# Four weight loads of a decoder layer moved ahead of its row loop, and the first block's schedule shifted by three rows

## The reference

```
z    = x @ W_in                                   # 9 sections of 1024 columns
o_A  = hgrn2_chunkwise(q, k, v, log f)            # 8 heads of 128
y_B  = cb * causal_depthwise_conv3(cc * ch)
mix  = (sigmoid(ga) * (o_A @ W_a) + sigmoid(gb) * (y_B @ W_b)) @ W_out
x1   = LayerNorm(alpha * x + mix)
x2   = LayerNorm(alpha * x1 + peer(x1))
out  = x2 + sigmoid(x2 @ W_pg) * (p @ W_pp)

peer(x1): for each token and each of 8 heads
  query = x1 @ W_q (2 halves of 128); scores against 2 x 128 keys
  top 16 of each half, 256 sums, top 16 of these -> 16 experts of 16384, softmax weights g
  result += sum_k g_k * gelu(u[e_k] . x1) * v[e_k]
```

## Time and profile before

| | |
|---|---|
| median of 3 runs | 1816.69 us (1812.79 to 1818.82) |
| the profiled execution | 1813.96 us |
| its span, first to last instruction | 1812.2 us |
| PE, DVE, ACT, POOL busy | 87%, 70%, 41%, 27% of the span |
| mean granted PE clock | 0.982 |
| moved by DMA | 655.37 MB, 362 GB/s over the span |

### The profile page before, as it was taken

One profiled execution on the slowest core, in us unless ns is written; L12 is line 12 of the kernel. 1 busy time (PEld: TensorE's weight loads), 2 busy tenths in 40 slices (PEclk: granted clock), 3 DMA queues, 4 the chain that ended last, 5 costly groups with the idle time before them and its releaser, 6 DMA issues.

```text
span 1812.2 us, 16782 instructions
## 1 busy us (share of the span) xinstructions
PE 1575.9 (87%) x4960; PEld 871.2 (48%) x4960; DVE 1275.4 (70%) x2750; ACT 747.9 (41%) x1899; POOL 496.0 (27%) x528
## 2 busy tenths in 40 slices
PE   8999989999999998889888668788787878877787
PEld 7888878776555566444344223332222223322224
DVE  4454475388998999678878876876666687666653
ACT  6566672222132224444334334444444443444432
POOL 0000000022222223233334433433333333333330
PEclk9999999999999999999999989999999999999999
DMA  5112368899999999999999999999999999999993
GB/s 203 70 65 93 113 262 343 294 415 398 421 420 421 417 397 418 406 415 412 421 421 411 422 416 422 391 420 423 421 412 422 410 410 422 421 421 422 420 418 138
DMA packets 94788, 655.37 MB, mean 362 GB/s; under 512 B 10352, under 2 KB 14192, under 8 KB 17008
## 3 DMA queue, kind: packets, MB, share of 16 engines
q0 software_dynamic: 73728, 536.90, 71.7%
q1 hardware_dynamic: 20976, 117.48, 16.7%
HBM read 652.24 MB, written 2.10 MB: 361 GB/s over the span
## 4 chain that ended last, share of the span: by engine, by line
PE 50%; DMA 30%; DVE 8%; ACT 8%; issue 3%; POOL 0%; SPq 0%; POOLq 0%; DVEq 0%; ACTq 0%
DMA uv<-in_pk_uv,idx 28%; PE psum L1703 12%; PE psum L1609 11%; PE psum L1467 10%; PE psum L1628 5%; DVE uv L1319 4%; PE psum L1671 4%; PE psum L1642 2%; PE psum L1580 2%; ACT diag L867 2%; ACT coef L859 1%; ACT L855 1%; ACT L833 1%; DMA raw<-in_w_in 1%; PE psum L1733 1%
## 5 line engine op out<-in xcount | busy, mean ns | idle before, releaser
L1703 PE MATMUL psum<-uv,diag 128*128 128x512 f32 x1440 | 721.0, 630 | 209.7 <-ACT diag L867 206.3
L632 POOL DMA_INDIRECT uv<-in_pk_uv,idx x512 | 493.6, 964 | 1279.8 <-PE psum L1703 583.1
L1319 DVE CUSTOM_DVE_ANT_0 uv<-uv,psum 128x1024 f32<-128x1024 f32 x512 | 623.2, 1218 | 310.5 <-DMA uv<-in_pk_uv,idx 304.1
L1703 PEld LDWEIGHTS psum<-uv,diag 128*128 128x128 f32 x1440 | 258.9, 195 | 644.8 <-ACT diag L867 426.8
L855 ACT ACTIVATE gelu<-dots 128x1 f32<-128x1 f32 x512 | 103.6, 202 | 780.7 <-DVE dots L1319 778.4
L1609 PE MATMUL psum<-xT,raw 128*128 128x384 f32 x640 | 208.1, 486 | 0.0
L1332 DVE SCALAR_TENSOR_TENSOR oT<-uv,coef,oT 128x1024 f32<-128x1024 f32 x148 | 189.3, 1279 | 3.0 <-ACT coef L859 3.0
L1609 PEld LDWEIGHTS psum<-xT,raw 128*128 128x128 f32 x640 | 120.9, 190 | 82.2
L859 ACT ACTIVATE coef<-gelu,weight 128x1 f32<-128x1 f32 x512 | 150.9, 295 | 16.6
L867 ACT ACTIVATE diag<-ident,coef 128x128 f32<-128x128 f32 x360 | 144.6, 402 | 11.8
L1467 PE MATMUL psum<-xTh,w_hi 128*128 128x512 f32 x256 | 105.0, 410 | 2.6 <-DVE xTl L1046 2.6
(11 more groups left out here) (204 smaller groups left out, 1576.7 us busy)
## 6 DMA issues: line engine op xcount, KB each, us to landing
raw<-in_w_in SPq DMA_DIRECT2D x40, 1024.0 KB, 7.8
raw_a<-in_w_a SPq DMA_DIRECT2D x12, 1024.0 KB, 4.7
raw<-in_pk_w_q SPq DMA_DIRECT2D x10, 1024.0 KB, 9.1
raw<-in_w_branch_a SPq DMA_DIRECT2D x8, 1024.0 KB, 8.0
raw<-in_w_branch_b SPq DMA_DIRECT2D x8, 1024.0 KB, 9.0
uv<-in_pk_uv,idx POOLq DMA_INDIRECT x512, 10.3
raw<-in_w_out SPq DMA_DIRECT2D x6, 1024.0 KB, 9.6
raw_w<-in_pk_w_q SPq DMA_DIRECT2D x6, 1024.0 KB, 6.0
```

The costliest lines, as they stand in the source:

```text
L632: pool.indirect_dma_start(uv[:, r % UV, :], None, pk_uv, bass.IndirectOffsetOnAxis(idx[:, i % 2, j:j + 1], 0)).then_inc(row_in[r % UV], 16)
L1319: V.tensor_tensor_reduce(u, u, x_cur[:], 1.0, 0.0, ALU.mult, ALU.add, dots[:, r % 32:r % 32 + 1]).then_inc(dot_done, 1)
L1703: last = T.matmul(B[i][:], diag[:, n % DR, :], uv[:, r % UV, D + i * 512:D + (i + 1) * 512], start=(r in FIRST), stop=(k == BLOCK_ROWS - 1 ...
```

## The change

Eight units, 4 to 11 (loads 2 to 5 before), are loaded as three transfers by `tri_fetch` behind query load 2 of block 0: three units into `gaT[:, :, 128:]`, three into `gbT[:, :, 128:]`, two into a part of `scores`. The host lays their columns out as `w_tri`. PE reads these units from there. The remaining unit loads are 6 to 19: load 6 where load 2 was, load 7 where load 3 was, load 8 where load 4 was. Load 9 waits for unit 15, loads 10 and 11 for unit 17, and load n from 12 on for unit 2(n - 3) + 1 as before. Query load 3 is issued with the third transfer, ahead of load 6.

The 38 late units are spread over 61 rows; merges and outputs start 3 rows later with the same spacing, so the last output row is 96. The norms and transposes keep their distance to it. `Q0` lies one row behind the last transpose rather than two, query 1 takes 5 rows instead of 6, and the scores of queries 0 and 1 come one row behind instead of two. Search 8 does three steps in a row instead of two. Of the rows behind the outputs, 106 isn't shared any more.

```diff
+        TRI0 = 4
+        tri = [gaT[:, :, P:], gbT[:, :, P:], scores[:, 0, :, P:3 * P]]
+        TRI1 = TRI0 + 8
...
             if i == PKH:
-                return [SCORE_ROW[0] + 2 + k // 2 for k in range(STEPS)]
+                return [SCORE_ROW[0] + 2 + k // 3 for k in range(STEPS)]
...
-        UNIT_ROW += [[(UNIT_MM * n + i) * 58 // (UNIT_MM * (len(UNITS) - EARLY)) for i in range(UNIT_MM)]
+        UNIT_ROW += [[(UNIT_MM * n + i) * 61 // (UNIT_MM * (len(UNITS) - EARLY)) for i in range(UNIT_MM)]
                      for n in range(len(UNITS) - EARLY)]
-        MERGE_ROW = [58 + n * 23 // 128 for n in range(16 * KT)]
-        OUT_ROW = [83 + n * 11 // 96 for n in range(4 * (TB - 1) * KT)]
+        MERGE_ROW = [61 + n * 23 // 128 for n in range(16 * KT)]
+        OUT_ROW = [86 + n * 11 // 96 for n in range(4 * (TB - 1) * KT)]
...
-        Q0 = TURN_ROW[-1] + 2
-        QUERY_ROW = [[Q0 + (n * 5 // 16 if h == 0 else 6 + n * 6 // 16 if h == 1 else 17 + 14 * (h - 2) + n * 9 // 16)
+        Q0 = TURN_ROW[-1] + 1
+        QUERY_ROW = [[Q0 + (n * 5 // 16 if h == 0 else 5 + n * 5 // 16 if h == 1 else 17 + 14 * (h - 2) + n * 9 // 16)
                       for n in range(2 * KT)] for h in range(PKH)]
-        SCORE_ROW = [QUERY_ROW[h][-1] + 2 for h in range(PKH)]
+        SCORE_ROW = [QUERY_ROW[h][-1] + (1 if h < 2 else 2) for h in range(PKH)]
...
-                return r % 3 == 1 and 106 <= r <= 120
+                return r % 3 == 1 and 109 <= r <= 120
...
-        LOADS += [(("unit", n), n - 2 if n < 4 else (n - 2) % 3) for n in range(2, len(UNITS) // 2)]
+        LOADS += [(("unit", n), n - TRI1 // 2 if n < 9 else (n - 8) % 3) for n in range(TRI1 // 2, len(UNITS) // 2)]
...
+            def tri_fetch(j):
+
+                sp.dma_start(tri[j], w_tri[j, :, :, 0:tri[j].shape[2]]).then_inc(tri_in[j], 16)
...
             fetch(pk_w_q[2], "query", 0, 2)
+            sp.wait_ge(t_done, USE["z", len(Z_PARTS) - 1] + 1)
+            tri_fetch(0)
+            tri_fetch(1)
+            sp.wait_ge(t_done, USE["query", 0, 0, 1] + 1)
+            fetch(pk_w_q[3], "query", 0, 3)
+            tri_fetch(2)
             sp.wait_ge(t_done, USE["unit", 1] + 1)
-            unit_fetch(2)
-            for h in (3, 4, 5):
+            unit_fetch(TRI1 // 2)
+            for h in (4, 5):
                 sp.wait_ge(t_done, USE["query", 0, h - 3, 1] + 1)
                 fetch(pk_w_q[h], "query", 0, h)
             sp.wait_ge(t_done, USE["unit", 3] + 1)
-            unit_fetch(3)
+            unit_fetch(TRI1 // 2 + 1)
...
-            for n in range(4, len(UNITS) // 2):
-                if n == 4:
+            for n in range(TRI1 // 2 + 2, len(UNITS) // 2):
+                if n == TRI1 // 2 + 2:
                     sp.wait_ge(t_done, USE["query", 0, 5, 1] + 1)
-                elif n < 7:
-                    sp.wait_ge(t_done, USE["unit", 2 * (n - 3) + 1] + 1)
                 else:
-                    sp.wait_ge(t_done, USE["unit", 2 * (n - 3) + 1] + 1)
+                    sp.wait_ge(t_done, USE["unit", 2 * max(n - 3, min(n - 2, 8)) + 1] + 1)
                 unit_fetch(n)
-                if n == 8:
+                if n == 9:
                     sp.wait_ge(t_done, USE["query", 0, PKH - 1, 1] + 1)
-                if 8 <= n < 8 + TB:
-                    first_parts(n - 7)
+                if 9 <= n < 9 + TB:
+                    first_parts(n - 8)
...
-                    pe.wait_ge(*loaded("unit", n // 2))
+                    if TRI0 <= n < TRI1:
+                        pe.wait_ge(tri_in[(n - TRI0) // 3], 16)
+                    else:
+                        pe.wait_ge(*loaded("unit", n // 2))
```

More of the change, by code:

```diff
@@ L30, with build @@
 CW = 2 * P
-def build(nc, x, x_t, p_t, w_a, w_in, vec_cols, w_branch_a, w_branch_b, w_out,
+def build(nc, x, x_t, p_t, w_a, w_in, w_tri, vec_cols, w_branch_a, w_branch_b, w_out,
           ln1_g, ln1_b, pk_w_q, sub_keys_t, pk_uv, ln2_g, ln2_b, ple_w_gate, ple_w_proj, out):
@@ L208, in build @@
         xT_in = sem("xT_in")
+        tri_in = [sem(f"tri_in{j}") for j in range(len(tri))]
         yc0_step, yc0_done, mix_step = sem("yc0_step"), sem("yc0_done"), sem("mix_step")
@@ L1605, in unit_mm @@
                         pe.wait_ge(xT_in, 16)
-                    pe.wait_ge(*loaded("unit", n // 2))
+                    if TRI0 <= n < TRI1:
+                        pe.wait_ge(tri_in[(n - TRI0) // 3], 16)
+                    else:
+                        pe.wait_ge(*loaded("unit", n // 2))
                     t_free(r)
-                half = n % 2
-                last = T.matmul(B[bank(r)][:, 0:SEQ - P], slot(SLOT["unit", n // 2])[:, k, half * P:half * P + P],
+                if TRI0 <= n < TRI1:
+                    w, part = tri[(n - TRI0) // 3], (n - TRI0) % 3
+                else:
+                    w, part = slot(SLOT["unit", n // 2]), n % 2
+                last = T.matmul(B[bank(r)][:, 0:SEQ - P], w[:, k, part * P:part * P + P],
                                 xT[:, k, P:], start=(k == 0), stop=(k == KT - 1), skip_group_check=True)
@@ L1869 @@
     w_a = w_in[[1, 0, 2, 3]].reshape(4, -1, P, w_in.shape[3], 2, P).transpose(0, 1, 2, 4, 3, 5)
+    sections = [(sect, c) for pair in range(4) for sect in (6, 5, 4) for c in (2 * pair, 2 * pair + 1)][4:12]
+    columns = [w_in[sect, c // 2][:, :, c % 2 * P:c % 2 * P + P] for sect, c in sections]
+    columns.append(columns[-1])
+    w_tri = _np.stack([_np.concatenate(columns[3 * j:3 * j + 3], axis=2) for j in range(3)])
     laid = {
@@ L1875 @@
         "w_in": w_in[4:],
+        "w_tri": w_tri,
         "vec_cols": _np.concatenate([_columns(given[name]) for name in
```

## The result

The changed kernel takes 1829.29 us (median of 6 runs, 1826.49 to 1832.23) against 1814.88 us before: 1.0075 times, 95% interval 1.0063 to 1.0087. That is 14.4 us slower, where 1809.9 us was forecast. The profiled execution is the slowest of the six (1832.23 us, span 1830.5), 18.3 us above the profiled one of before.

What follows compares the result with a forecast made beforehand. The DMA is full, but PE's fixed work paces the rows up to 705 us and gathers alone thereafter. Terms -7.5 + 0.3 + 0.4 = -6.8 us took the median 1816.69 to 1809.9 us; range 1805.5 to 1817.0.

Steps and rivals of the forecast that it cites:

- rival E: Unit stage: loads 9 and 10 take 16.0 us each, PE stands 5.7 us twice; 5.9 us slower, 1822.6 us; chance 0.09.
- PE ends the output chunks at 705 us again, but with row 96 in place of row 93 behind it: From 366 to 705 us: PE's fixed work ends unchanged with 3 more rows beneath it, the main term, 7.5 us less.
- It just fits by the sum.: From 340 to 366 us, ahead of the rows: at 421 GB/s the DMA has room for the 4.19 MB more.
- Rival D: Start of the rows: at 362 GB/s only 2.65 MB fit, query 4 is 4.2 us late; 1813.4 us; chance 0.07.
- I take 0.3 us late; bounds 0 and 4.2 us.: Start of the rows: query load 4, reckoned to land at 365.3 us with 0.8 us margin, costs 0.3 us.
- VectorE starts behind by 2 us and has 8.7 us of free time ... to make it good.: First dots to 455 us: VectorE's late start of 2 us is absorbed in 8.7 us of free time, without PE waiting.
- After, with a DMA that is not full, some 27 can be landed by then.: By 455 us: some 27 gathers landed, leaving 52.4 MB against 52.2 MB to 579 us, a lag under a microsecond.
- rival B: From 400 to 455 us: the ring of six buffers is full and the DMA idles; 1813.0 us; chance 0.14.
- So both make it by 0.4 us.: Unit stage: loads 9 and 10, with leads cut to 10.3 us, land just in time; 0.4 us taken for both.
- Behind 705 us, 3 rows fewer are to be gathered, ... 7.5 us less.: Behind the output chunks: 3 rows fewer at 2.49 us each, 7.5 us less.
- Rival C, VectorE becomes the bound: Rows before 705 us: VectorE's 9 us of added work is hidden only by half, 4 us lost; 1813.3 us; chance 0.08.
- I cost all this at nothing, bounds -1 and +2.5 us.: End of block 0: closer queries and denser search 8 stay hidden, at no cost, bounds -1 and +2.5 us.

Runs made afterwards that it cites:

- rows_only: The kernel before with the change's 61 unit rows, later merges and outputs and drawn-together end of block 0, but the old loads: 1820.25 us, 1.0028.
- tail_only: The kernel before with only the end of block 0 (queries, scores, search 8) drawn together as in the change: 1818.23 us, 1.0022.
- late58x: The kernel before with the new loads, query load 4 right behind query load 3, third transfer and load 6 behind query load 7: 1816.35 us, 1.0011.
- late61: The change with third transfer, load 6 and four half loads moved behind query load 7, query load 4 right behind query load 3: 1818.39 us, 1.0022.
- loads_only: The kernel before with the change's three early transfers and shorter leads, but the old rows and end of block 0: 1821.54 us, 1.0036.
- late58: As late58x, with the four half loads (x of blocks 1 to 3, norm gain) also issued right behind query 7: 1815.01 us, 1.0001.
- late59: As late58, with 59 unit rows instead of 58, and merges and outputs one row later: 1814.92 us, 1.0004.

## Why the prediction was wrong, point by point

The change came out slower, at 1829.29 us, where the range ended at 1817.0 us and even rival E gave only 1822.6. The main step that failed is "PE ends the output chunks at 705 us again, but with row 96 in place of row 93 behind it": they ended at 720.9 us, as PE began its late units late and waited 8.3 us for VectorE's merge of row 85. The points below follow the prediction from the start of the rows on.

**"It just fits by the sum."** The first step that failed. It reckoned with 421 GB/s ahead of the rows; the stretch moved 368. At that rate the room is (368 - 260) x 26 = 2.8 MB, not 4.19. More than half of the (421 - 368) x 26 = 1.4 MB that are missing lies before the new loads could flow: from 340 to 344 us the DMA moved 223 GB/s, as in the kernel before (225), since the first transfer is issued only at 342.74 us. That is (421 - 223) x 4 = 0.8 MB. The 374 GB/s of the first two transfers make 0.4 MB. Rival D had about the right price here (362 GB/s, 2.65 MB) and too small a chance, but partly by luck: its 362 GB/s mixed the end of two gain loads with pieces of 512 B, landed by 328.0 us, with a load of 8 KB runs; the load with 1.5 KB pieces had landed at 319.4 us. The Trainium skill (DMA: Bandwidth & Descriptors, Bandwidth, "Where 436 GB/s comes from") has 358 GB/s for one core's loads from HBM. The 374 GB/s of the first two transfers lie near it, but loads with 8 KB runs ran at 421 in the same kernel, so its limit is not what the trace shows. The size of the pieces fits, with `xT`'s 372 GB/s beside it (two loads agree; no run changed the size alone).

**"I take 0.3 us late; bounds 0 and 4.2 us."** Query 4 landed at 371.40 us where 365.3 was reckoned, and PE waited 3.9 us. That is within the bound. Of the 6.1 us, 2.3 were there when the second transfer landed, 1.6 came up to the third (364.3 us), and 2.2 with query 4 itself, which took 4.7 us behind load 6 with gathers under way, where 2.5 was reckoned. What the bound left out is the clock: the query took 6.56 us for 3.74 at a granted clock of 0.53 from 370 to 375 us, 2.8 us more. The late units began 8.1 us later; 6.7 are these two, the rest lay ahead of 366 us.

**"VectorE starts behind by 2 us and has 8.7 us of free time ... to make it good."** It started 3.4 us behind. The free time was not free in the way needed: VectorE waits for PE's convolution units there (6.8 us, one wait of 4.5; 2.6 was the longest before), and the ring of six rows was full meanwhile (POOL waited up to 7.8 us for VectorE's sum).

**"After, with a DMA that is not full, some 27 can be landed by then."** Only 26 were issued by 455 us, against 27 before, and 24 had landed. From 420 to 440 us the DMA left (421 - 273) x 10 + (421 - 145) x 10 = 4.2 MB unmoved, as much as the change took out of the rows. This is rival B's idling, and with it the 455 to 579 us stretch was again full, with more in it: rows 34 to 59 waited 14.7 us for their gathers, where it was 10.1 before, and took 89.9 us for 84.2. The budget of bytes was right as a sum and wrong in the place: a ring of six buffers can't store what the DMA has to spare.

**"So both make it by 0.4 us."** Right, for loads 9 and 10: 9.3 and 9.5 us of 10.3, and no wait on PE. The 0.4 us of the sum were nothing, and load 9 was issued 8 us later than reckoned.

**The merges.** The prediction read the chain as "three pieces without a break". The 1.28 us of "issue" between the merges and the output chunks were a break, and it is the one that grew. The prediction costed merges and outputs as keeping "their density" and named no wait. The largest single term was here: PE's wait for VectorE's last merge, 8.3 us against 1.3, because row 85 isn't reached when PE has done the same work. Its dot began at 673.07 us, 14.4 us later than row 82's before (658.70), and the merges ended only 7.2 us later. Without the new loads (rows_only) the wait was still 5.9 us, so most of it comes from the three rows themselves. With 1.7 us of slower output chunks behind the wait, its 7.0 us more make 8.7 us of the 16.0 by which the outputs end late; 7.2 are from the start.

**"Behind 705 us, 3 rows fewer are to be gathered, ... 7.5 us less."** This term was right: it fits within 0.2 us in six kernels at row 110. But it counts from the end of PE's outputs, and these came 16.0 us later.

**Rival C, VectorE becomes the bound,** was priced at 4 us and given 0.08 (with the sum's own 0.7 us for the start and the leads its terms give 1813.9 us, not 1813.3). It is nearer to what happened than the forecast (VectorE is busy 9.9 to 10.0 of every 10 us from 610 to 700 us after the change), but its way to the end is PE's wait, not its own length.

**The end of block 0: "I cost all this at nothing, bounds -1 and +2.5 us."** Measured alone 4.0 us (tail_only; interval 2.2 to 5.6), outside the bounds for the most part. The search, for which the prediction named a wait, shows no cost. What costs most is the start of the queries one row behind the last transpose.

**Rival E** (loads 9 and 10 late) had the right sign and the wrong cause. PE has no wait on a load among the late units.

**The sum as measured:** +7.2 (units) + 7.0 (wait) + 1.7 (clock in the outputs) - 7.5 (rows) = +8.4 us at row 110 (measured 8.3). The end of block 0 adds about 4. The rest, some 2 us of the median, lies in rows 110 to 180, where the change is behind by 10 more us in its profiled execution than at row 110; no run tells that part apart. It may be no more than this one execution: late58x, with rows and end of before, loses 5.6 us there in its profile. Why `Q0` one row earlier costs what it does, which of block 0's last jobs collides with it, stays open too.

## What to carry to other kernels

Where one engine does fixed work beneath a loop of another, ask what that engine waits for at each change of stage before stretching its work over more rounds of the loop: a wait that is tied to a round number moves with it, and here 1.3 us became 8.3. Bytes taken out of a full stretch are worth something only if what they leave room for can be issued; with a small ring that is bounded by the consumer, and a lead from elsewhere (loads moved into the hole, as in late61) has to fill it. Before a prefetch is put ahead of a latency chain, reckon the queue in front of the next small load that the chain needs, at the rate of the pieces it will really move.

## What the hardware showed that was not expected

Transfers with pieces of 1.5 KB moved at 374 GB/s (and `xT` at 372) with no gather beside them, where loads with 8 KB runs and gathers of 8 KB move 421. In a wait from 367.6 to 371.4 us PE's granted clock fell: it was 0.53 from 370 to 375 us, about the lower of its two levels (1.2 of 2.4 GHz), and the 32 matmuls behind the wait took 6.56 us for 3.74. So a wait of 3.9 us cost PE 6.7. The 8.3 us wait at 669 us went with 0.71 from 670 to 680 us and output chunks that took 1.7 us longer. Waits of 1.3 us at the same place (before, loads_only, late58, late59) left them at 41.7 us, and one of 3.1 us (late61) made them 43.4. The Trainium skill (TensorE: Matmul & The Clock Gate, Part 1) has a gate that passes fewer clock pulses depending on how busy PE has been, and the trace agrees: 0.53 of the clock behind a stretch without work.
